# A two-part transformer kernel: scaled activations split straight from x, and SBUF tiles placed at chosen distances modulo 512 bytes

## The chip, the cores and the metric

One core of one Trainium2 chip. The metric is the device time of one execution in microseconds, median of three runs. Everything is computed on one NeuronCore; weights, 353 MB of them with the other inputs, are streamed from HBM once.

## The reference

Two blocks in sequence on x of 256 positions by 1024 features in fp32, each block with two layers. Cut to what matters here:

```
# first block, per layer
x = x + 0.5 * swiglu(rmsnorm(x, ffn1_norm), w_up, w_down)
x = x + mixer(rmsnorm(x, mix_norm), ...)      # attention, conv module, gates, w_out
x = x + 0.5 * swiglu(rmsnorm(x, ffn2_norm), w_up, w_down)
x = rmsnorm(x, final_norm)
# second block, per layer
p = rmsnorm(x, norm1) @ w_in                  # K, Q, V and the Fourier part
x = x + concat(rmsnorm(fourier), rmsnorm(attention)) @ w_o
x = x + (silu(gate) * val) @ w_down           # of conv3(rmsnorm(x, norm2) @ w_up)
```

## The kernel before

**Precision by parts.** Each product of activations and weights is made of three matmuls in fp32r. A number is split into a high part (rounded to fp32r) and a low part (the rest). `mm3` (lines 443 to 445) multiplies w_hi by a_hi, w_hi by a_lo and w_lo by a_hi, in this order, into one PSUM bank. Each matmul loads its own weights first (128 by 128) and moves 256 columns of activations. While a matmul moves its columns, the weights of the next are loaded.

**The weight stream.** SyncE loads chunks of 2048 fp32 per partition (half of that for some) into `raw`, with three slots. ScalarE copies a chunk into `hi` (line 1066), VectorE writes `lo` = `raw` - `hi` (line 1618), and TensorE works through it: 48 matmuls on a full chunk, 24 on a half one. A slot of `hi` and `lo` is free when TensorE is done with it, a slot of `raw` when VectorE has written `lo`.

**The stages.** In each of the six feed-forward blocks (FFN) TensorE takes 33 chunks: the moving tiles are `n_hi` and `n_lo` for the way up, `hid_hi` and `hid_lo` for the way down, and `last_*` and `end_*` for the last chunks down. A layer of the first block then has value chunks (moving 512 columns of weights), eight GLU chunks, twelve of queries and keys, two of values, eight of gates (moving tiles `h_hi`, `h_lo`), the projections (`yt_*`, `s_*`) and w_out (`h_*` again). The second block's projection w_o also moves `h_*`. While the queries, keys and gates are computed, VectorE makes the depthwise convolution of 31 taps on 8 tiles: `conv_taps` is a generator of single taps, and the constants `TAPS_GLU`, `TAPS_QK`, `TAPS_V` and `TAPS_HEAD` say how many are made in each step. `TAPS_HEAD[t]` belongs to step t of the gate stage, in which one pair of heads is also attended to.

**The seams.** Where a matmul chain ends in x, `add_to_x` (line 1719) adds two PSUM halves to a pair p of x's eight tiles. The next norm's gain is applied to x, and the result is split: VectorE writes x times gain into a wide tile (`scale_x`, line 1677; `fused_scale`, line 1662, with two gains where the final norm lies between), ScalarE copies it to `n_hi` (`scaled_high`, line 1111), VectorE subtracts (`scaled_low`, line 1622). The division by the root mean square comes later, out of the PSUM bank, so TensorE can start on a pair of `n_hi` and `n_lo` as soon as it is there. ScalarE also squares x for the statistic (`squares`, line 1115), and at the two fused seams, behind the first block's layers, makes a second set of squares (`psq`, line 1098). There are 40 such pairs; the 8 ahead of the mixer keep the wide tile, since it is used again.

**The layout.** `sb` (in `build`) hands out SBUF addresses one behind the other, in multiples of 64 bytes. All tiles that matter here have rows of a multiple of 512 bytes, so each has one distance modulo 512 from the base of `hi`: before, `raw`, `lo`, `x`, `h_hi`, `h_lo` and `sq` are at 0, `last_*` and `end_*` at 128, `n_*`, `hid_*`, `s_*` and `yt_*` at 192.

Of the kernel before, what the change touches and what calls it, by code (L numbers as in the profile page):

```python
# [20 lines left out]
F32 = mybir.dt.float32  # L21
# [9 lines left out]
L = 2  # L31
# [13 lines left out]
TAPS_HEAD = (14, 12, 16, 20, 20, 8 * 31, 0, 0)  # L45
# [155 lines left out]
def _stream(chunks):  # L201
    return dict(hi=chunks, lo=chunks, pe=chunks, slot=chunks, load0=16 * chunks // 3,
                load1=16 * chunks // 3, load2=16 * chunks // 3)


def _ffns(n):
    return dict(half=n * (PAIRS - 1), up=n * JT, silu=n * JT, prod=n * JT, hidhi=n * JT, hid=n * JT,
                dpair=3 * n)
# [4 lines left out]
    added2=16 * ADDED_IN[2], x=12, sq=12, stat=3, std=3, h32=16, hhi=16, h=16, prm=1,  # L213
# [5 lines left out]
    _stream(CHUNKS2), **_ffns(1), x=8, sq=8, ssum=2, stat=2, std=2, h32=8, hhi=8, h=8, prm=1,  # L219
# [5 lines left out]
class Semaphores:  # L225
# [6 lines left out]
             "yf", "fsum", "fstat", "fstd", "mf", "wo", "fgain", "psq", "plink", "psum", "pstat", "pstd", "minus", "added0", "added1", "added2")  # L232


def build(nc, d):
# [61 lines left out]
    spread = sb("spread", [P, 2 * ROWS * HD], F32, at_u + (KT * UPW + KT * S) * 4 + 10240)  # L297
    at_t = state["at"]
# [44 lines left out]
    nmx, den, rden, fgain, nsink = (small[:, 16 * i:16 * i + 16] for i in range(5))  # L343

# [707 lines left out]
    def act_program(act):  # L1052
# [33 lines left out]
        def fused_input(p, l):  # L1086

            scaled_high(p)
            take("x")
            if l == 0 and p == 0:  # L1090
                act.wait_ge(sem["fgain"], L + 1)
            for t in (2 * p, 2 * p + 1):
                out, src = xsq[:, t, :], x[:, t, :]
                if l == L - 1:
                    out, src = natural(out), evens_first(src)
                last = fn(out, src, ACT.Square, scale=fgain[:, l * KT + t:l * KT + t + 1])
            last.then_inc(sem["sq"], 1)
            fn(psq[:, 2 * p:2 * p + 2, :], x[:, 2 * p:2 * p + 2, :], ACT.Square).then_inc(sem["psq"], 1)
# [13 lines left out]

        def squares(p):
            take("x")
            fn(xsq[:, 2 * p:2 * p + 2, :], now["x"][:, 2 * p:2 * p + 2, :], ACT.Square).then_inc(sem["sq"], 1)

        def projection(c0, half):

            for m in range(KT):
                split(c0 + m + 2, half(c0 + m + 2))  # L1120
                take("pe")
                if m % 2 == 0 and m:
                    scaled_input(m // 2 - 1)
            scaled_input(3)
# [118 lines left out]
        def first_inputs():  # L1243

            scaled_high(0)
            first_high(0)
            scaled_high(1)
            first_high(1)
            scaled_high(2)
            scaled_high(3)  # L1250
            act.wait_ge(load[1], 16)
            fn(hi[:, 1, :], raw[:, 1, :], ACT.Copy).then_inc(sem["hi"], 1)
            for p in range(4):
                squares(p)
            take("prm")

        def layer1(l):
            if l == 0:
                first_inputs()
            else:  # L1260
                for p in range(4):
                    fused_input(p, l - 1)
                take("prm")
# [215 lines left out]

        def layer2(l):  # L1480
            for p in range(4):
                if l == 0:
                    fused_input(p, L - 1)
                else:
                    scaled_input(p)
# [77 lines left out]
            scaled_input(0)  # L1563
            take("pe")
            split(B_FFN0)
            scaled_input(1)
            take("pe")
            split(B_FFN0 + 1)
            scaled_input(2)
            take("pe")  # L1570
            scaled_input(3)
# [23 lines left out]
    def dve_program(v):  # L1595
# [57 lines left out]
        def fused_scale(p, l):  # L1653

            take("x")
            at = l * NP1 + P1["final"]
            next_at = (l + 1) * NP1 + P1["ffn1"] if l < L - 1 else L * NP1 + P2["norm1"]
            for t in (2 * p, 2 * p + 1):
                out, part = sq[:, t, :], x[:, t, :]
                if l == L - 1:  # L1660
                    out, part = natural(out), evens_first(part)
                last = v.tensor_scalar(out, part, prm_all[:, at + t:at + t + 1], prm_all[:, next_at + t:next_at + t + 1],
                                       ALU.mult, ALU.mult)
            last.then_inc(sem["h32"], 1)

        def gain_of(table, gain, t):
            if table is P2 and gain == "norm1":
                at = L * NP1 + now["layer"] * NP2 + P2["norm1"] + t
                return prm_all[:, at:at + 1]
            return col(table, gain, t)  # L1670

        def scale_x(p, table, gain):

            take("x")
            for j in range(2):
                t = 2 * p + j
                last = v.tensor_scalar(now["wide"][:, t, :], now["x"][:, t, :], gain_of(table, gain, t), None, ALU.mult)  # L1677
            last.then_inc(sem["h32"], 1)

        def scaled_low(p):  # L1680
            take("hhi")
            low_part(n_lo[:, 2 * p:2 * p + 2, :], now["wide"][:, 2 * p:2 * p + 2, :], n_hi[:, 2 * p:2 * p + 2, :], "h")

# [72 lines left out]
        def projection(c0, half, factor, table, gain):  # L1756

            for m in range(KT - 1):
                split(c0 + m + 2, half(c0 + m + 2))
                if m % 2:  # L1760
                    v.wait_ge(sem["pe"], pe_after(c0 + m))
                    add_to_x(OUT_BANKS[m // 2], m // 2, factor)
                    scale_x(m // 2, table, gain)
                elif m:
                    scaled_low(m // 2 - 1)
            v.wait_ge(sem["pe"], pe_after(c0 + KT - 1))
            add_to_x(OUT_BANKS[3], 3, factor)
            scale_x(3, table, gain)
            split(c0 + KT + 1, half(c0 + KT + 1))
            scaled_low(3)  # L1770
# [121 lines left out]
        def first_inputs():  # L1892

            def arrived(p):
                v.wait_ge(sem[f"xld{p}"], 16)
                v.sem_inc(sem["x"], 1)
                scale_x(p, P1, "ffn1")

            v.wait_ge(sem["gains"], 16)
            arrived(0)  # L1900
            scaled_low(0)
            arrived(1)
            first_low(0)
            scaled_low(1)
            arrived(2)
            first_low(1)
            scaled_low(2)
            arrived(3)
            scaled_low(3)
            v.wait_ge(sem["hi"], 2)  # L1910
            v.tensor_tensor(lo[:, 1, :], raw[:, 1, :], hi[:, 1, :].bitcast(F32), ALU.subtract).then_inc(sem["lo"], 1)
            v.wait_ge(sem["prmld"], 16)
            v.tensor_copy(prm[:, 0:NP1], prm_all[:, 0:NP1]).then_inc(sem["prm"], 1)
            v.wait_ge(sem["prm"], 1)

        def layer1(l):
            start["pe"] = cnt.at("pe")

            if l:
                v.tensor_copy(prm[:, 0:NP1], prm_all[:, l * NP1:(l + 1) * NP1]).then_inc(sem["prm"], 1)  # L1920
                take("prm")
            else:
                cnt.up("prm")
            roped["rope"] = cnt.at("rope")
# [144 lines left out]
            projection(WOUT0, half_chunk_1, 0.5, P1, "ffn2")  # L2069
# [14 lines left out]
        def ffn2(cb):  # L2084
# [57 lines left out]
            if now["layer"] < L:  # L2142
                scaled_residual(c + 6, 1.0, P2, "norm1")
            else:
                residual(c + 6, 1.0)
                cnt.up("x", 4)
                cnt.up("hhi", 4)
# [74 lines left out]

        def pair_done(p):
            add_to_x(OUT_BANKS2[p], p, 1.0)
            scale_x(p, P2, "norm2")

        def layer2(l):
# [91 lines left out]
            scaled_low(0)  # L2319
# [3 lines left out]
            scaled_low(1)  # L2323
# [4 lines left out]
            scaled_low(2)  # L2328
            scaled_low(3)
# [222 lines left out]
```

## Time and profile before

| | us |
|---|---|
| median of three runs | 1968.24 |
| the three runs | 1968.24, 1966.21, 1976.1 |
| the profiled execution, its own time | 1977.89 |
| its span, first to last instruction | 1976.1 |
| TensorE busy in the span | 1928.1 |
| VectorE busy | 1498.7 |
| ScalarE busy | 1082.2 |

The profile is of one execution, which took 1977.89 us, 9.65 us more than the median of the runs. TensorE's busy time holds overlaps: a matmul's record lasts about 0.28 us although the next starts some 0.12 us after it, so the pace of matmuls is read from their starts, or from their number in a stretch.

### The profile page before, as it was taken

What the parts mean: (1) busy time and instruction counts of PE and PEld (TensorE: products, weight loads), DVE (VectorE), ACT (ScalarE), POOL (GpSimd) and SP (SyncE); (2) the same over time, 40 slices, a digit from 0 to 9 for tenths busy, and PEclk for the clock granted to TensorE, in tenths of its full rate; (3) what the DMA queues carried; (4) which work ended last, traced back from release to release, by engine and by line L of the source; (5) the groups of instructions that cost most, each with busy time, mean ns of one, the idle gap of its engine ahead of it and who ended that gap; (6) DMA issues with size and microseconds to landing.
All of it is one profiled execution on the core that took longest, in us unless ns stands there. A gap on an engine that the chain in (4) does not pass through costs nothing.

```text
span 1976.1 us, 38819 instructions
## 1 busy us (share of the span) xinstructions
PE 1928.1 (98%) x15828; PEld 1857.7 (94%) x15828; DVE 1498.7 (76%) x2189; ACT 1082.2 (55%) x1370; POOL 31.4 (2%) x40
## 2 busy tenths in 40 slices
PE   6999999999999999999999999999999999999998
PEld 6999899889999999998988899999889999889998
DVE  6555889987765586668898877555888778879777
ACT  4444556666544464445666665444665555566554
POOL 0000001000000000000110000000000000000000
PEclk9999999999999999999999999999999999999999
DMA  6556579634655545555896246555335554435554
GB/s 240 204 183 227 184 236 275 173 89 140 212 194 189 191 162 200 191 209 187 256 257 171 84 149 227 198 179 188 110 126 192 191 191 171 138 130 175 187 187 143
DMA packets 61003, 362.28 MB, mean 183 GB/s; under 512 B 7904, under 2 KB 8160, under 8 KB 24160
## 3 DMA queue, kind: packets, MB, share of 16 engines
q1 hardware_dynamic: 54704, 339.37, 49.5%
q0 software_dynamic: 5184, 18.88, 5.5%
q10 hardware_dynamic: 1008, 2.51, 0.3%
q8 instruction: 79, 1.29, 0.3%
q14 instruction: 28, 0.23, 0.0%
HBM read 353.39 MB, written 1.05 MB: 179 GB/s over the span
## 4 chain that ended last, share of the span: by engine, by line
PE 76%; DVE 15%; ACT 5%; DMA 2%; issue 1%; DVEq 0%; ACTq 0%; SPq 0%
PE bank L443 24%; PE bank L444 23%; PE bank L445 23%; DVE lo L1618 5%; DVE cv L1862 3%; ACT hi L1066 2%; DMA raw<-in_w 1%; DVE n_lo L1622 1%; PE bank L585 1%; DMA x<-in_x 1%; DMA lo<-in_w 1%; DVE p_sb L1841 1%; PE bank L607 0%; DVE up_t L1698 0%; DVE sq L1677 0%
## 5 line engine op out<-in xcount | busy, mean ns | idle before, releaser
L1618 DVE TENSOR_TENSOR lo<-raw,hi 128x2048 fp32r<-128x2048 f32 (+1 forms) x336 | 676.6, 2015 | 203.0 <-ACT hi L1066 202.5
L443 PE MATMUL bank<-n_hi,hi 128*128 128x256 f32 x2256 | 638.2, 283 | 24.7 <-DVE lo L1889 12.7
L1066 ACT ACTIVATE hi<-raw 128x2048 fp32r<-128x2048 f32 (+1 forms) x336 | 598.3, 1783 | 110.5 <-PE bank L445 92.2
L444 PE MATMUL bank<-n_lo,hi 128*128 128x256 f32 x2256 | 631.3, 280 | 0.0
L445 PE MATMUL bank<-n_hi,lo 128*128 128x256 f32 x2256 | 631.1, 280 | 0.0
L443 PEld LDWEIGHTS bank<-n_hi,hi 128*128 128x128 f32 x2256 | 427.9, 190 | 31.5 <-DVE lo L1889 12.7
L444 PEld LDWEIGHTS bank<-n_lo,hi 128*128 128x128 f32 x2256 | 426.6, 189 | 1.3 <-issue 1.0
L445 PEld LDWEIGHTS bank<-n_hi,lo 128*128 128x128 f32 x2256 | 426.5, 189 | 0.0
L443 PE MATMUL bank<-h_hi,hi 128*128 128x256 f32 x1152 | 335.9, 292 | 5.0 <-DVE h_lo L1622 4.3
L444 PE MATMUL bank<-h_lo,hi 128*128 128x256 f32 x1152 | 327.1, 284 | 0.0
L445 PE MATMUL bank<-h_hi,lo 128*128 128x256 f32 x1152 | 326.9, 284 | 0.0
L443 PE MATMUL bank<-hid_hi,hi 128*128 128x256 f32 x928 | 259.5, 280 | 0.5 <-DVE lo L1618 0.5
L445 PE MATMUL bank<-hid_hi,lo 128*128 128x256 f32 x928 | 259.2, 279 | 0.0
L444 PE MATMUL bank<-hid_lo,hi 128*128 128x256 f32 x928 | 259.2, 279 | 0.0
L443 PEld LDWEIGHTS bank<-h_hi,hi 128*128 128x128 f32 x1152 | 221.7, 192 | 17.9 <-issue 12.6
L444 PEld LDWEIGHTS bank<-h_lo,hi 128*128 128x128 f32 x1152 | 222.2, 193 | 0.5
L445 PEld LDWEIGHTS bank<-h_hi,lo 128*128 128x128 f32 x1152 | 222.0, 193 | 0.0
L1132 ACT ACTIVATE silu_t<-up_t 128x256 f32<-128x256 f32 x88 | 36.8, 418 | 298.3 <-DVE up_t L1698 298.3
L1862 DVE SCALAR_TENSOR_TENSOR cv<-upad,prm,cv 128x256 f32<-128x256 f32 x480 | 195.4, 478 | 0.0
L443 PEld LDWEIGHTS bank<-hid_hi,hi 128*128 128x128 f32 x928 | 175.5, 189 | 0.9 <-DVE lo L1618 0.9
L444 PEld LDWEIGHTS bank<-hid_lo,hi 128*128 128x128 f32 x928 | 174.9, 189 | 0.0
L445 PEld LDWEIGHTS bank<-hid_hi,lo 128*128 128x128 f32 x928 | 174.8, 188 | 0.0
(257 smaller groups left out, 2302.4 us busy)
## 6 DMA issues: line engine op xcount, KB each, us to landing
raw<-in_w SPq DMA_DIRECT2D x286, 1024.0 KB, 4.8
raw<-in_w SPq DMA_DIRECT2D x53, 512.0 KB, 4.0
lo<-in_w POOLq DMA_DIRECT2D x36, 512.0 KB, 9.0
zt<-zt SPq DMA_DIRECT2D x96, 64.0 KB, 5.8
bv<-in_bv SPq DMA_DIRECT2D x2, 768.0 KB, 6.1
spread<-in_spread SPq DMA_DIRECT2D x2, 768.0 KB, 8.0
x<-in_x ACTq DMA_DIRECT2D x4, 256.0 KB, 10.4
out_x<-sq SPq DMA_DIRECT2D x1, 1024.0 KB, 3.9
```

Of the source, the lines that this page charges most:

```text
L443: mm(out, w_hi, a_hi, start=start, stop=False, skip_group_check=True)
L444: mm(out, w_hi, a_lo, start=False, stop=False, skip_group_check=True)
L445: return mm(out, w_lo, a_hi, start=False, stop=True, skip_group_check=True)
L585: last = mm(bank[7][j * HD:(j + 1) * HD, 0:S], const[:, w:w + HD], zgsq[:, j, :], start=(m == 0), stop=(m == QK_CHUNKS - 1), skip_group_ch ...
L1066: fn(hi[:, s, 0:w], raw[:, s, 0:w], ACT.Copy).then_inc(sem["hi"], 1)
L1132: fn(silu_t[:, u, :], gate_of[:, u, 0, :], ACT.Silu).then_inc(sem["silu"], 1)
L1618: v.tensor_tensor(lo[:, s, 0:w], raw[:, s, 0:w], hi[:, s, 0:w].bitcast(F32), ALU.subtract)\
L1622: return v.tensor_tensor(out, full, high.bitcast(F32), ALU.subtract).then_inc(sem[name], 1)
L1841: v.tensor_tensor_reduce(p_sb[:, e, :], bank[3 + e][:, :], mask_f[:, u % 2, :], -(HD ** -0.5), 3e38, ALU.add, ALU.min, nmx[:, i:i + 1]).th ...
L1862: ins = v.scalar_tensor_tensor(cv[:, t, :], src, w, cv[:, t, :], ALU.mult, ALU.add)
```

## The change

It has four parts.

1. **Layout.** `lo` moves to 256 modulo 512 from `hi`; `x`, `h_hi`, `h_lo` and `sq` move to 192; `z`, `zt`, `p_sb`, `last_*`, `end_*` and what shares their place move from 128 to 192. `raw`, `hi`, `n_*`, `hid_*`, `s_*`, `yt_*`, and the constants stay where they were modulo 512.
2. **Parts straight from x.** For 32 of the 40 pairs the wide tile is gone: `direct_high` makes `n_hi` as x times gain on ScalarE, in two instructions of one tile each, and `direct_low` makes `n_lo` as (x times gain) minus `n_hi` on VectorE, again in two. The product of the two gains of a fused seam, `seam_gain`, is computed once at the start, by two small instructions on VectorE.
3. **Order on ScalarE at the fused seams.** The squares of pair p come behind the high part of pair p+1, and the second squares (`psq`) behind all of them.
4. **Taps.** `TAPS_HEAD` goes from (14, 12, 16, 20, 20, rest) to (14, 12, 16, 18, 18, 18, rest).

The programs of TensorE, SyncE and GpSimd are the same instructions in the same order.

```diff
-TAPS_HEAD = (14, 12, 16, 20, 20, 8 * 31, 0, 0)
+TAPS_HEAD = (14, 12, 16, 18, 18, 18, 8 * 31, 0)
...
     raw = sb("raw", [P, SLOTS, CW], F32)
     hi = sb("hi", [P, SLOTS, CW], F32R)
+    state["at"] += 256
     lo = sb("lo", [P, SLOTS, CW], F32R)
+    state["at"] += 256
+    state["at"] += 192
     x = sb("x", [P, KT, S], F32)
     h_hi = sb("h_hi", [P, KT, S], F32R)
     h_lo = sb("h_lo", [P, KT, S], F32R)
     sq = sb("sq", [P, KT, S], F32)
+    state["at"] += 320
     const = sb("const", [P, C["mask1"]], F32)
...
     spread = sb("spread", [P, 2 * ROWS * HD], F32, at_u + (KT * UPW + KT * S) * 4 + 10240)
+    state["at"] += 64
     at_t = state["at"]
...
+        def fused_inputs(l):
...
+            for p in range(4):
+                direct_high(p, x, lambda t: seam_gain[:, l * KT + t:l * KT + t + 1], l == L - 1)
+                if p:
+                    final_squares(p - 1)
+            final_squares(3)
+            for p in range(4):
+                fn(psq[:, 2 * p:2 * p + 2, :], x[:, 2 * p:2 * p + 2, :], ACT.Square).then_inc(sem["psq"], 1)
...
+        def direct_high(p, src, gain, in_order=False):
+
+            take("x")
+            for t in (2 * p, 2 * p + 1):
+                out, part = n_hi[:, t, :], src[:, t, :]
...
+                last = fn(out, part, ACT.Copy, scale=gain(t))
+            last.then_inc(sem["hhi"], 1)
...
+        def direct_low(p, src, gain, in_order=False):
+
+            take("x")
+            take("hhi")
+            for t in (2 * p, 2 * p + 1):
+                out, part, high = n_lo[:, t, :], src[:, t, :], n_hi[:, t, :].bitcast(F32)
...
+                last = v.scalar_tensor_tensor(out, part, gain(t), high, ALU.mult, ALU.subtract)
+            last.then_inc(sem["h"], 1)
...
         def fused_residual(c, factor, l):
+
+            def low(p):
+                direct_low(p, x, lambda t: seam_gain[:, l * KT + t:l * KT + t + 1], l == L - 1)
...
                 add_to_x(2 + p, p, factor)
-                fused_scale(p, l)
                 if p:
-                    scaled_low(p - 1)
-            scaled_low(3)
+                    low(p - 1)
+            low(3)
```

The other places (`projection`, `direct_residual`, the second block's four pairs ahead of its FFN, and the first inputs) are changed in the same way.

On VectorE, at the seam behind the first layer, the rows before, from the first `add_to_x` to the first low part (the last three rows stand twice more, and then one more low part):

```order
L1719 SCALAR_TENSOR_TENSOR x<-bank,x 128x512
L1662 TENSOR_SCALAR sq<-x,prm_all 128x256 x2
L1719 SCALAR_TENSOR_TENSOR x<-bank,x 128x512
L1662 TENSOR_SCALAR sq<-x,prm_all 128x256 x2
L1622 TENSOR_TENSOR n_lo<-sq,n_hi 128x512
```

and in the changed kernel:

```order
L1746 SCALAR_TENSOR_TENSOR x<-bank,x 128x512 x2
L1708 SCALAR_TENSOR_TENSOR n_lo<-x,small,n_hi 128x256 x2
L1746 SCALAR_TENSOR_TENSOR x<-bank,x 128x512
L1708 SCALAR_TENSOR_TENSOR n_lo<-x,small,n_hi 128x256 x2
L1746 SCALAR_TENSOR_TENSOR x<-bank,x 128x512
L1708 SCALAR_TENSOR_TENSOR n_lo<-x,small,n_hi 128x256 x4
```

The four scalings are gone, and each low part is two instructions of one tile that read x, the gain (in `small`) and `n_hi`; the second `add_to_x` follows the first at once.

On ScalarE at the same seam, the last two chunks of the FFN and the first pair before (the other three pairs are alike):

```order
L1066 ACTIVATE hi<-raw 128x2048 x2
L1111 ACTIVATE n_hi<-sq 128x512
L1096 ACTIVATE xsq<-x,small 128x256 x2
L1098 ACTIVATE psq<-x 128x512
L1111 ACTIVATE n_hi<-sq 128x512
```

and all of it in the changed kernel, with the chunk that follows:

```order
L1134 ACTIVATE n_hi<-x,small 128x256 x4
L1103 ACTIVATE xsq<-x,small 128x256 x2
L1134 ACTIVATE n_hi<-x,small 128x256 x2
L1103 ACTIVATE xsq<-x,small 128x256 x2
L1134 ACTIVATE n_hi<-x,small 128x256 x2
L1103 ACTIVATE xsq<-x,small 128x256 x4
L1112 ACTIVATE psq<-x 128x512 x4
L1072 ACTIVATE hi<-raw 128x2048
```

The high parts of the first two pairs now come ahead of any squares, and `psq` moved from between the pairs to their end, ahead of the copy of the next chunk.

On VectorE in the first layer's gate stage, the head of step 6 before (steps 3 to 5 end in runs of 20, 20 and 18 taps, `SCALAR_TENSOR_TENSOR cv<-upad,prm,cv`; the ISA rows are the minima over scores and their read-out):

```order
L1618 TENSOR_TENSOR lo<-raw,hi 128x2048
L1846 RECIPROCAL small<-small 128x2
L1841 ISA p_sb,small<-bank,mask_f 128x512
L1841 ISA small 128x1
L1841 ISA p_sb,small<-bank,mask_f 128x512
```

and in the changed kernel (where steps 3 to 5 have 18, 18 and 18):

```order
L1653 TENSOR_TENSOR lo<-raw,hi 128x2048
L1885 RECIPROCAL small<-small 128x2
L1901 SCALAR_TENSOR_TENSOR cv<-upad,prm,cv 128x256 x4
L1880 ISA p_sb,small<-bank,mask_f 128x512
L1880 ISA small 128x1
```

Four taps moved behind the reciprocal of step 6.

## Rows read from the trace of the kernel before

**Rows 1.** Page: engines, granted clock in 40 slices, chain's shares

```profile
PE 1928.1 (98%) x15828; PEld 1857.7 (94%) x15828; DVE 1498.7 (76%) x2189; ACT 1082.2 (55%) x1370; POOL 31.4 (2%) x40
...
PEclk9999999999999999999999999999999999999999
...
PE 76%; DVE 15%; ACT 5%; DMA 2%; issue 1%; DVEq 0%; ACTq 0%; SPq 0%
```

**Rows 2.** Windows, TensorE: stretch, us, busy us (instructions), clock, DMA share, GB/s

```profile
40.00:190.00 150.00, 150.00 (x1274) 1.00 0.58 204
540.00:690.00 150.00, 150.00 (x1276) 1.00 0.55 191
735.00:870.00 135.00, 135.00 (x1193) 1.00 0.58 207
1220.00:1370.00 150.00, 150.00 (x1276) 1.00 0.55 194
1525.00:1655.00 130.00, 130.00 (x1150) 1.00 0.56 198
1815.00:1955.00 140.00, 140.00 (x1191) 1.00 0.54 185
230.00:270.00 40.00, 40.00 (x334) 1.00 0.56 188
1158.00:1170.00 12.00, 12.00 (x108) 1.00 0.66 206
1960.00:1970.00 10.00, 10.00 (x86) 1.00 0.07 29
```

**Rows 3.** Timeline at 750 us: start us, us, engine, line, operation

```profile
749.91 0.19 PEld L444 LDWEIGHTS bank<-n_lo,hi 128*128 128x128 f32 x1
750.02 0.28 PE L444 MATMUL bank<-n_lo,hi 128*128 128x256 f32 x1
750.03 0.19 PEld L445 LDWEIGHTS bank<-n_hi,lo 128*128 128x128 f32 x1
```

**Rows 4.** Windows, all engines: PE, PEld, DVE, ACT, POOL, then as above

```profile
272.00:345.00 73.00, 73.00 (x586) 67.63 (x586) 67.94 (x128) 50.30 (x65) 9.50 (x11) 1.00 1.02 283
382.00:428.00 46.00, 44.76 (x391) 41.49 (x390) 43.22 (x104) 31.50 (x55) 2.59 (x3) 1.00 0.49 123
490.00:514.00 24.00, 23.56 (x196) 23.36 (x196) 16.77 (x25) 11.64 (x14) 0.00 (x0) 1.00 0.72 230
```

**Rows 5.** Timeline of VectorE at the second seam

```profile
1390.46 0.68 DVE L1719 SCALAR_TENSOR_TENSOR x<-bank,x 128x512 f32<-128x512 f32 x1
1391.17 0.74 DVE L1662 TENSOR_SCALAR sq<-x,prm_all 128x256 f32<-128x256 f32 x2
1391.83 0.68 DVE L1622 TENSOR_TENSOR n_lo<-sq,n_hi 128x512 fp32r<-128x512 f32 x1
1392.82 0.69 DVE L1622 TENSOR_TENSOR n_lo<-sq,n_hi 128x512 fp32r<-128x512 f32 x1 [0.31 <-ACT n_hi L1111]
1393.43 2.28 DVE L1618 TENSOR_TENSOR lo<-raw,hi 128x2048 fp32r<-128x2048 f32 x1
```

**Rows 6.** Timeline of ScalarE there

```profile
1392.17 0.61 ACT L1111 ACTIVATE n_hi<-sq 128x512 fp32r<-128x512 f32 x1
1392.69 0.92 ACT L1096 ACTIVATE xsq<-x,small 128x256 f32<-128x256 f32 x2
1393.51 0.61 ACT L1098 ACTIVATE psq<-x 128x512 f32<-128x512 f32 x1
```

**Rows 7.** Waits of TensorE on `n_lo`: us, times, longest

```profile
PE bank L443 <- DVE n_lo L1622: 5.5, 8, 1.7
```

**Rows 8.** Chain of waits in a gate stage: start us, us, what

```profile
415.78 7.91 DVE cv L1862 x20
...
427.19 7.12 DVE cv L1862 x18
...
438.61 1.27 PE bank L635 x8
```

More of the change, by code:

```diff
@@ L1084, in final_gains, with final_squares @@
             fn(fgain, fgain, ACT.Sqrt, bias=eps).then_inc(sem["fgain"], 1)
[L1086 to L1090, printed above, removed]
+        def fused_inputs(l):
+            if l == 0:
                 act.wait_ge(sem["fgain"], L + 1)
[L1092 to L1098, printed above, removed]
+                act.wait_ge(sem["seam"], L)
+            def final_squares(p):
+                for t in (2 * p, 2 * p + 1):
+                    out, src = xsq[:, t, :], x[:, t, :]
+                    if l == L - 1:
+                        out, src = natural(out), evens_first(src)
+                    last = fn(out, src, ACT.Square, scale=fgain[:, l * KT + t:l * KT + t + 1])
+                last.then_inc(sem["sq"], 1)
+            for p in range(4):
[5 more added lines that the diff above has]
+                fn(psq[:, 2 * p:2 * p + 2, :], x[:, 2 * p:2 * p + 2, :], ACT.Square).then_inc(sem["psq"], 1)
         def final_std(out, src, seam):
@@ L1111, in scaled_high, with direct_input @@
             fn(n_hi[:, 2 * p:2 * p + 2, :], now["wide"][:, 2 * p:2 * p + 2, :], ACT.Copy).then_inc(sem["hhi"], 1)
+        def direct_high(p, src, gain, in_order=False):
+            take("x")
+            for t in (2 * p, 2 * p + 1):
+                out, part = n_hi[:, t, :], src[:, t, :]
+                if in_order:
+                    out, part = natural(out), evens_first(part)
+                last = fn(out, part, ACT.Copy, scale=gain(t))
+            last.then_inc(sem["hhi"], 1)
+        def direct_input(p, gain):
+            direct_high(p, now["x"], gain)
+            fn(xsq[:, 2 * p:2 * p + 2, :], now["x"][:, 2 * p:2 * p + 2, :], ACT.Square).then_inc(sem["sq"], 1)
         def squares(p):
@@ L1260, in layer1 @@
             else:
-                for p in range(4):
-                    fused_input(p, l - 1)
+                fused_inputs(l - 1)
                 take("prm")
@@ L1651, in final_scale @@
                 last.then_inc(sem["plink"], 1)
[L1653 to L1670, printed above, removed]
         def scale_x(p, table, gain):
@@ L1676, in scale_x @@
                 t = 2 * p + j
-                last = v.tensor_scalar(now["wide"][:, t, :], now["x"][:, t, :], gain_of(table, gain, t), None, ALU.mult)
+                last = v.tensor_scalar(now["wide"][:, t, :], now["x"][:, t, :], col(table, gain, t), None, ALU.mult)
             last.then_inc(sem["h32"], 1)
@@ L1682, in scaled_low @@
             low_part(n_lo[:, 2 * p:2 * p + 2, :], now["wide"][:, 2 * p:2 * p + 2, :], n_hi[:, 2 * p:2 * p + 2, :], "h")
+        def direct_low(p, src, gain, in_order=False):
+            take("x")
+            take("hhi")
+            for t in (2 * p, 2 * p + 1):
+                out, part, high = n_lo[:, t, :], src[:, t, :], n_hi[:, t, :].bitcast(F32)
+                if in_order:
+                    out, part, high = natural(out), evens_first(part), natural(high)
+                last = v.scalar_tensor_tensor(out, part, gain(t), high, ALU.mult, ALU.subtract)
+            last.then_inc(sem["h"], 1)
         def summed_squares():
@@ L1754, in scaled_residual, with direct_residual, projection @@
             scaled_low(3)
-        def projection(c0, half, factor, table, gain):
+        def direct_residual(c, factor, gain):
+            for p in range(4):
+                if p < 3:
+                    take("dpair")
+                else:
+                    v.wait_ge(sem["pe"], pe_after(c))
+                add_to_x(2 + p, p, factor)
+                if p:
+                    direct_low(p - 1, now["x"], gain)
+            direct_low(3, now["x"], gain)
+        def projection(c0, half, factor, gain):
             for m in range(KT - 1):
@@ L1923, in layer1 @@
                 cnt.up("prm")
+                for m in range(L):
+                    at = m * NP1 + P1["final"]
+                    next_at = (m + 1) * NP1 + P1["ffn1"] if m < L - 1 else L * NP1 + P2["norm1"]
+                    v.tensor_tensor(seam_gain[:, m * KT:(m + 1) * KT], prm_all[:, at:at + KT],
+                                    prm_all[:, next_at:next_at + KT], ALU.mult).then_inc(sem["seam"], 1)
+                v.wait_ge(sem["seam"], L)
             roped["rope"] = cnt.at("rope")
@@ L2142, in ffn2 @@
             if now["layer"] < L:
-                scaled_residual(c + 6, 1.0, P2, "norm1")
+                at = L * NP1 + now["layer"] * NP2 + P2["norm1"]
+                direct_residual(c + 6, 1.0, lambda t: prm_all[:, at + t:at + t + 1])
             else:
@@ L2327, in layer2 @@
             pair_done(3)
-            scaled_low(2)
-            scaled_low(3)
+            direct_low(2, now["x"], norm2)
+            direct_low(3, now["x"], norm2)
             split(B_FFN0 + 1)
```

71 lines of the change are left out of this document (37 added, 34 removed).

## The prediction

> **What bounds the kernel now.** I read the page first, then TensorE's pace in windows, then the timeline for one pair of matmuls, and last the waits and the chain around the places that the change edits.
>
> TensorE is busy 98% of the span, has the full clock in every slice, and holds 76% of the chain that ended last [rows 1]. Waiting is a small part of the time, so the question is how fast TensorE goes while it does not wait. The windows of rows 2 answer that. A window also counts about two matmuls that started before it (a record is 0.28 us long), so I divide by the count less two. Every matmul in these windows moves 256 columns and loads 128 by 128 weights, yet there are three paces:
>
> - 117.8 ns in four of the six FFNs (windows at 40, 540, 1220 and 1815 us: 150 us / 1272 and alike), 113.3 ns in the other two (735 and 1525) and in the stage of `s_*` (1158): all of them move tiles at distance 192 from the base of `hi`;
> - 120.5 ns in the GLU stage (230), which moves `h_*` at distance 0;
> - 119 ns at the end (1960), where `last_*` and `end_*` lie at distance 128 [rows 2].
>
> The pace of an FFN holds through the whole block, whichever slot of weights is in use. Within a pace, the next weights start loading 10 ns after a matmul's start, and the matmul after starts when they are in [rows 3]: the two streams of reads run side by side all the time, and their relative place sets how much they cost each other. That is my reading. The trace shows no address, only that equal work has three paces and that the tile's distance goes with them. At 192 there are two paces, and which one holds looks like a matter of how the two streams fell in step after the last wait.
>
> **The layout, h and last tiles.** Moving `h_*` to 192 gives 120.5 - 113.3 = 7.2 ns per matmul if it takes the fast pace, 2.7 ns if the slow one, nothing if distance is not the cause.
> - GLU: 2 layers x 8 chunks x 48 = 768 matmuls, fast: 5.5 us.
> - Queries and keys: 2 x 12 x 48 = 1152, fast 8.3 us. VectorE is busy 67.94 of 73 us there and the DMA engines all of the time [rows 4]. Taking 4.1 us out of 73 would bring VectorE to 98.6%, so I count half: 4.2 us.
> - Gates: VectorE is busy 43.22 of 46 us [rows 4] and its taps are on the chain [rows 8]. Nothing from the pace.
> - w_out: the DMA share is 0.72 with half chunks [rows 4], and its chunks come late. I count nothing there, and half of 384 x 7.2 for w_o: 1.5 us.
> - `last_*` and `end_*`: 384 matmuls x (119 - 113.3) = 2.2 us.
>
> **The layout, low weights.** `lo` goes to 256. Then the matmuls that load high weights keep distance 192, and those that load low weights, one in three, get 192 - 256, which is 448 modulo 512. No row shows 448. The bounds come from rows 2: at best all three go at 113.3, at worst that one goes at 120.5 and takes the others to 117.8, or 118.7 on average. The jump of 256 comes twice in every three loads, so two streams that fell in step badly are put out of step again each time, while the fast pace costs the two streams nothing that a jump could take away. I take the fast pace, with doubt. Some 6,000 matmuls of the four slow FFNs are past their first, waiting chunks: 6,000 x (117.8 - 113.3) = 27.0 us. This is the largest term and the least certain one.
>
> The Trainium skill speaks against all of this: in "SBUF — State Buffer", section "Who interferes with whom", it gives TensorE two independent read ports and says that TensorE never waits on anyone. By that rule both layout terms are zero and the sum is 6.7 us. Rows 2 do not fit it: same work, same clock, 113.3 to 120.5 ns.
>
> **The seams.** A pair cost VectorE 0.68 + 0.74 + 0.68 us before, with starts 1.98 us apart per pair [rows 5]. It will cost the 0.68 us of `add_to_x` and two fused operations of one tile. Twenty taps of that kind and size take 7.91 us [rows 8], 0.40 each, so 0.8 us for two. That is 1.5 us per pair: about 0.5 less, 16 us of VectorE in all 32 pairs, nearly all beside TensorE's work. ScalarE pays: a copy of 0.61 us becomes two scaled ones, and the nearest row has two scaled squares at 0.92 [rows 6], so 0.3 more per pair, 10 us in all, under 55% load [rows 1]. At the fused seams `psq` now lies ahead of the next chunk's copy, but the pairs are earlier by more than it costs.
> What of this is on the path: TensorE waits for `n_lo` 8 times, 5.5 us in total [rows 7], and VectorE goes on serially to the next chunk's low part [rows 5] and the sum of squares. Following the new order through the second seam, the last low part ends 1.4 us earlier (four pairs at 0.5 less, less 0.6 since TensorE's own pairs now set the start), the first fused seam 1.3, the second block's inner seam 0.8, the two projections 0.2 each and the two w_o seams 0.3 each. Sum 4.5 us. The first inputs have the longer high part and the two small products in a serial chain: +0.4. Net 4.1 us. Ends: 0 (another wait takes its place) and the 5.5 of rows 7 plus the same again.
>
> **The taps.** In the gate stage the chain goes from 20 taps to 18 to a wait of TensorE [rows 8]. Four taps leave steps 3 and 4 (2 each), none is added to step 5, which had 18 of the rest anyway, and four come in step 6, after the last wait. That is 4 x 0.40 = 1.6 us per layer. They end near the sum over the tiles that needs them, so I count 1.3: 2.6 us.
>
> **The sum.** 27.0 + 5.5 + 4.2 + 1.5 + 2.2 + 4.1 + 2.6 = 47.1 us. Against the profiled execution's own time: 1977.9 - 47.1 = 1930.8, say **1931 us**. That execution is 9.7 us above the median of 1968.2. If its four slow FFNs are more than other runs have, my term is smaller against the median but ends at the same place, since all blocks are then fast. So 1931 stands for the median too.
>
> **The rivals.**
> - *The low part's shift does nothing* (0.30): if the streams meet again every 256 bytes or less, 448 is the same as 192. For it: the tiles at 0 and at 128 have nearly one pace [rows 2], which looks like a short period. Then FFNs fall to either pace as before, `h_*` and the last tiles too. The h terms shrink to about 4 of 7.2 ns: 3.1 + 2.3 + 0.8 + 1.2, with seams and taps 14.1 us: 1963.8 against the profiled execution, 1954.1 against the median. Named time: 1959.
> - *Slower: the low weights' matmuls go badly* (0.15): 448 is 64 from 0, and the pace at 0 is the worst one known [rows 2]. Today's mean over the 13,700 matmuls concerned is 117.3 ns (6336 at 117.8, 3456 at 120.5, 384 at 119, the rest 113.3). It decides above 117.8 ns, where it eats the 6.7 us of seams and taps. At 118.7 it costs 1.4 x 13,700 = 19 us less 6.7: 1990 against the profiled execution; half of that gives 1984, and 1974 against the median.
> - *Distance is not the cause* (0.10): the stage of `h_*` is slow for another reason, say its other traffic. Against it is rows 2, where `s_*`, at another distance in the same layer, goes at 113.3. Only the 6.7 us of seams and taps stay: 1971 against the profiled execution, 1962 against the median. The rule of the Trainium skill quoted above comes out here.
>
> **How the numbers follow.** My forecast has 0.45, with its own range 1921 (queries and keys gain in full, seams at their upper end) to 1943 (a fifth of the FFN term and half of the others missing). About 0.5%, or 10 us, is what a measurement can tell from no change: faster is under 1958.4, slower over 1978.1. Faster: 0.45, half of 0.30, and 0.03 of the rest: 0.63. Slower: 0.12 of the second rival. Same: 0.25. The range reaches from 1921 through the first and the last rival to 1970, leaving out mostly the second.
>
> **What would show it.** Right: every long FFN window at 113 ns, GLU there too, `n_lo` waits below 3 us, the last low part of the second seam 1.4 us closer to its first `add_to_x`, VectorE's busy time down by some 16 us and ScalarE's up by 10. Wrong: FFN windows still split between 113 and 118 (first rival), any steady pace above 118 (second), GLU still at 120.5 (third).

## The result and the profile after

| | before | after |
|---|---|---|
| median, us | 1971.08 (11 runs, 1966.21 to 1977.08) | 1960.52 (11 runs, 1952.08 to 1968.35) |
| profiled execution, its own time, us | 1977.89 | 1954.6 |
| its span, us | 1976.1 | 1952.8 |

The ratio of after to before is 0.9936, 95% interval 0.9918 to 0.9955: faster by 0.64%, or 10.6 us between the medians and 23.3 us between the profiled executions. The forecast was 47.1 us and 1931 us; the first rival (the shift of the low weights does nothing) had named 1959.

The page's lines for engines, clock and chain [rows 1]:

```profile
PE 1903.9 (97%) x15828; PEld 1833.5 (94%) x15828; DVE 1484.9 (76%) x2159; ACT 1091.1 (56%) x1402; POOL 31.4 (2%) x40
...
PEclk9999999999999999999999999999999999999999
...
PE 72%; DVE 19%; ACT 4%; DMA 3%; issue 2%; SPq 0%; DVEq 0%; ACTq 0%
```

VectorE's busy time fell by 13.8 us and ScalarE's rose by 8.9, about as forecast (16 and 10), and the clock is as before. TensorE's busy time fell by 24.2 us.

The windows of TensorE's pace answer to [rows 2] (stretch, us, busy us with the number of matmuls, clock, DMA share, GB/s): the six FFNs in order, then GLU, `s_*`, and the end tiles.

```profile
40.00:190.00 150.00, 150.00 (x1276) 1.00 0.58 205
530.00:680.00 150.00, 150.00 (x1275) 1.00 0.54 189
720.00:860.00 140.00, 139.59 (x1231) 1.00 0.58 203
1210.00:1360.00 150.00, 150.00 (x1276) 1.00 0.55 191
1510.00:1640.00 130.00, 130.00 (x1150) 1.00 0.56 199
1795.00:1930.00 135.00, 135.00 (x1193) 1.00 0.57 196
230.00:268.00 38.00, 37.82 (x333) 1.00 0.60 200
1145.00:1157.00 12.00, 12.00 (x108) 1.00 0.69 207
1937.00:1946.00 9.00, 8.65 (x75) 1.00 0.12 52
```

The FFNs still have the two paces, 117.8 ns (150 us / 1274) and 113.3 to 113.9. Three are slow instead of four. GLU went from 120.5 to 114.8 ns by the window (38 us / 331, small waits included), and the last tiles from 119 to 118.5 or less (8.65 us / 73). The mean distance of starts inside blocks, with waits left out, says it sharper. Outside the gates, where attention comes in between, `h_*` had 119.8 to 119.9 ns before in all six stretches, and has 113.3 to 117.8 after: the two stretches of w_o, in the second block, took the slow pace. `last_*` and `end_*` of the last FFN together had 119.9 before and have 115.5 after.

The second seam on VectorE [rows 5], its first row before:

```profile
1385.13 0.68 DVE L1719 SCALAR_TENSOR_TENSOR x<-bank,x 128x512 f32<-128x512 f32 x1
```

and after:

```profile
1370.94 0.68 DVE L1746 SCALAR_TENSOR_TENSOR x<-bank,x 128x512 f32<-128x512 f32 x1
1372.05 0.69 DVE L1746 SCALAR_TENSOR_TENSOR x<-bank,x 128x512 f32<-128x512 f32 x1 [0.42 <-PE bank L451]
1372.70 0.88 DVE L1708 SCALAR_TENSOR_TENSOR n_lo<-x,small,n_hi 128x256 fp32r<-128x256 f32 x2
...
1377.05 0.88 DVE L1708 SCALAR_TENSOR_TENSOR n_lo<-x,small,n_hi 128x256 fp32r<-128x256 f32 x2 [0.68 <-ACT n_hi L1134]
```

and on ScalarE [rows 6]:

```profile
1375.23 0.92 ACT L1103 ACTIVATE xsq<-x,small 128x256 f32<-128x256 f32 x2
1376.03 0.91 ACT L1134 ACTIVATE n_hi<-x,small 128x256 fp32r<-128x256 f32 x2
```

From the start of the first `add_to_x` to the end of the last low part it took 8.38 us before (1385.13 to 1393.51) and takes 6.99 (1370.94 to 1377.93): 1.39 us less, where 1.4 was forecast. The last low part now waits for ScalarE, which spends 0.92 + 0.91 us per pair; a pair's low part is 0.88 us on VectorE, not 0.8. TensorE's waits on low parts of `n` [rows 7] went from 8 times, 5.5 us, to:

```profile
PE bank L449 <- DVE n_lo L1657: 2.0, 1, 2.0
...
PE bank L449 <- DVE n_lo L1708: 1.2, 4, 0.6
```

That is 3.2 us in all, where the forecast's sign was below 3. Other waits grew: on `lo` from 6.7 us to

```profile
PE bank L449 <- DVE lo L1653: 8.2, 10, 1.4
```

The chain in the first gate stage [rows 8]:

```profile
412.17 7.12 DVE cv L1901 x18
...
422.79 7.12 DVE cv L1901 x18
...
434.21 1.27 PE bank L641 x8
```

The long runs of taps are 7.12 us each, so the one of 7.91 is shorter by 0.79. What TensorE's faster pace did in the stage of queries and keys is seen in the windows of all engines (columns as in [rows 4]):

```profile
272.00:343.00 71.00, 68.79 (x571) 62.70 (x569) 65.78 (x124) 50.06 (x64) 8.64 (x10) 1.00 1.01 276
```

TensorE was busy in all of its window before, and now stands still for 2.2 of 71 us; VectorE is at 93% and the DMA engines still at all of the time. The chain changed hands. Its shares there, before (272 to 345 us):

```profile
by line: PE bank L443 32.1%; PE bank L444 29.6%; PE bank L445 29.5%; PE bank L585 7.2%; PE bank L596 1.7%
```

After, the transfers of `zt` hold 29.6% of the chain in 272 to 345 us, where they had no share before. Three of its pieces (start us, us, what):

```profile
279.96 10.36 DMA zt<-zt
290.34 1.24 DVE zt L1864
...
312.27 11.27 DMA zt<-zt
```

**Where the time went.** Stage lengths from the starts of records, the two layers of the first block (GLU from its first matmul to its last sigmoid, queries and keys to the last copy of `zt`, gates from there to the last `yt_hi`):

| stage, us | before | after | layout alone | parts and taps alone |
|---|---|---|---|---|
| GLU | 46.4, 46.3 | 44.2, 43.8 | 44.2, 43.8 | 46.4, 46.3 |
| queries, keys | 79.2, 80.0 | 78.8, 77.9 | 76.8, 76.3 | 79.1, 79.1 |
| gates | 101.7, 101.7 | 100.7, 101.8 | 101.8, 101.7 | 100.1, 100.1 |
| w_out, to the next FFN's first matmul | 25.6, 24.0 | 23.3, 23.3 | 24.9, 24.0 | 23.5, 24.1 |

The difference of the two spans is 23.3 us. GLU gave 4.7, queries and keys 2.5, gates 0.9, w_out 3.0, the stretches behind the two fused seams (their start to the next `h` matmul) 1.4 and 1.5, the second block's inner seam 0.8, w_o 1.2, the start with the first FFN 0.8, in sum 16.8. The last FFN gave 5.5 (176.8 to 171.3, up to its `last_*` tiles), and this need not be the change's: e8 below shows the same step in the kernel before. The last 1.0 us is spread over the rest.

### The profile page after: what moved, and what is told of

It is laid out like the page before. It is cut to its first block, busy times and chain, and to the rows that moved or that the text cites. A ratio compares the mean times of both kernels' runs of the same rounds, so it can differ in the third digit from the quotient of the medians.

```text
span 1952.8 us, 38855 instructions
## 1 busy us (share of the span) xinstructions
PE 1903.9 (97%) x15828; PEld 1833.5 (94%) x15828; DVE 1484.9 (76%) x2159; ACT 1091.1 (56%) x1402; POOL 31.4 (2%) x40
## 4 chain that ended last, share of the span: by engine, by line
PE 72%; DVE 19%; ACT 4%; DMA 3%; issue 2%; SPq 0%; DVEq 0%; ACTq 0%
PE bank L449 23%; PE bank L450 22%; PE bank L451 22%; DVE lo L1653 6%; DVE cv L1901 5%; DMA zt<-zt 2%; ACT hi L1072 1%; DVE zt L1864 1%; ACT n_hi L1134 1%; DMA raw<-in_w 1%; DVE qk L1874 1%; DVE p_sb L1880 1%; PE bank L613 0%; DVE c L2122 0%; DVE c L2118 0%
## 5 line engine op out<-in xcount | busy, mean ns | idle before, releaser
L449 PE MATMUL bank<-h_hi,hi 128*128 128x256 f32 x1152 | 330.1, 287 | 7.3 <-DVE h_lo L1657 3.9
L451 PE MATMUL bank<-h_hi,lo 128*128 128x256 f32 x1152 | 321.1, 279 | 0.0
L450 PE MATMUL bank<-h_lo,hi 128*128 128x256 f32 x1152 | 321.1, 279 | 0.0
L450 PEld LDWEIGHTS bank<-h_lo,hi 128*128 128x128 f32 x1152 | 217.9, 189 | 0.5
```

The costliest lines, as they stand in the source:

```text
L449: mm(out, w_hi, a_hi, start=start, stop=False, skip_group_check=True)
L450: mm(out, w_hi, a_lo, start=False, stop=False, skip_group_check=True)
L451: return mm(out, w_lo, a_hi, start=False, stop=True, skip_group_check=True)
```

## The experiments

All numbers "per block" are mean distances of the starts of neighbouring matmuls of 256 columns, waits left out, from the trace of the profiled execution; those of `h_*` leave out the gates. e4 to e11 and e13 to e15 are single executions, on several chips, so their paces say more than their times: single executions of the kernel before beside e5 to e11 took 1970.84 and 1980.69 us.

**e1: layout alone.** The kernel before with the four shifts of the change.

```diff
# before.py
+    state["at"] += 256      # ahead of lo
+    state["at"] += 448      # ahead of x
+    state["at"] += 320      # ahead of const
+    state["at"] += 64       # ahead of z
```

> The kernel before with the layout part of the change alone (lo at 256, h, x, sq and the last tiles at 192). Theory 1, distance sets the pace and the low part's shift does nothing: GLU windows at 113.3 or 117.8 ns instead of 120.5, FFN blocks still at either 113.3 or 117.8, time 5 to 9 us below the kernel before. Rival, the tiles' distance is not the cause and all of the change's gain is its shorter seams and taps: GLU still at 120.5 and no difference in time.

1962.54 us, ratio 0.9929 (0.9903 to 0.9954). FFNs: 117.7, 117.6, 113.8, 117.7, 117.6, 113.8 ns; `h_*` 113.3 to 114.2 in five stretches and 117.8 in one. So the move of the `h` tiles works, and four FFNs are slow again.

**e2: parts and taps alone.** The changed kernel with the old layout.

```diff
# after.py
-    state["at"] += 256
...
-    state["at"] += 256
-    state["at"] += 192
...
-    state["at"] += 320
...
-    state["at"] += 64
```

> The changed kernel with the old layout: the parts straight from x, the order on ScalarE and the taps alone. Theory 1: GLU at 120.5 ns again, the two fused seams as short as in the changed kernel, time 4 to 8 us below the kernel before. Rival, the gain is the layout's alone: no difference to the kernel before.

1966.57 us, ratio 0.9945 (0.9918 to 0.9972). `h_*` is at 119.8 to 119.9 ns everywhere, where e1 has the fast pace in them: together they end the rival that distance is not the cause. Four of the six FFNs are slow here too (117.6 to 117.7 ns). The gates give 1.6 us per layer (table above), which is the taps' 4 x 0.40; parts and taps were not run apart.

**e3: no shift of the low weights.** The changed kernel with `lo` at 0; all else stays at its place.

```diff
-    state["at"] += 256
     lo = sb("lo", [P, SLOTS, CW], F32R)
-    state["at"] += 256
     state["at"] += 192
```

> The changed kernel with lo at 0 instead of 256 modulo 512, all else as in it. Theory 1, the shift does nothing: the same two paces, the same time as the changed kernel within 4 us. Rival, the shift helps some blocks into the fast pace: more blocks at 117.8 and a time 5 us or more above the changed kernel; or it hurts: a time below it.

1955.27 us, ratio 0.9902 (0.9881 to 0.9923), no worse than with the shift. The FFNs: 113.4, 117.8, 117.8, 117.6, 113.5, 113.6 ns. Three are slow, as in the changed kernel, and the two profiled executions took 1955.24 and 1954.6 us. The shift by 256 bought nothing. The medians are 5.3 us apart, more than the 4 us expected; whether the shift even costs something is open. The first, second and third FFN:

```profile
40.00:190.00 150.00, 150.00 (x1326) 1.00 0.59 211
530.00:680.00 150.00, 150.00 (x1276) 1.00 0.55 190
720.00:860.00 140.00, 140.00 (x1191) 1.00 0.57 199
```

**e4 to e7: the distance by itself.** All moving tiles at one distance D, `lo` at 0, with 256, 64, 448, 128 for D.

```diff
     hi = sb("hi", [P, SLOTS, CW], F32R)
-    state["at"] += 256
     lo = sb("lo", [P, SLOTS, CW], F32R)
-    state["at"] += 256
-    state["at"] += 192
+    state["at"] += D
```

The pad of 320 ahead of `const` stays as it is, and carries `n_*`, `hid_*` and all later moving tiles from 192 to D as well. The constants and other tiles shift with them.

> The changed kernel with lo at 0 and every moving tile at distance 256 from hi (one look, for the pace). If the two streams of reads meet again every 256 bytes or less, 256 is the same as 0: all blocks at 120.5 ns, time near 2000 us. If they meet every 512 bytes, 256 is the farthest from 0: a pace of its own, at 113.3 or below, time under 1950 us.

> All moving tiles at 64 modulo 512 from hi, lo at 0, parts and taps as changed. Theory A (the streams meet again every 256 bytes, and the distance from a meeting decides): 64 has the same distance as 192 on the other side; paces of 113.3 and 117.8 ns per block again, about 1955 to 1962 us. Theory B (the sign counts, moving tile ahead of the weights by 64 is worse or better): one single pace, between 110 and 120 ns, in every block: at 113.3 everywhere 1925 to 1935 us, at 119 to 120 about 1995 us.

> All moving tiles at 448 modulo 512 from hi, lo at 0. Theory A (period 256): the same as 192, so FFN blocks and h blocks at 113.3 or 117.8 ns and 1952 to 1965 us. Theory B (period 512): another pace than at 192, at worst 120 ns and 2000 us. This is the distance that the low weights' matmuls have in the change.

> All moving tiles at 128 modulo 512 from hi, lo at 0. Theory A (period 256, 128 is furthest from a meeting): like last_* and end_* of the kernel before, 118.7 to 119.9 ns everywhere, about 1990 us. Theory B (the distance from a meeting alone decides, the further the faster): below 117 ns everywhere, under 1950 us.

| D | time, us | paces per block, ns |
|---|---|---|
| 256 | 2000.0 | 120.0 in every FFN, 119.8 to 120.0 in `h_*` |
| 64 | 1969.4 | 117.8 in five FFNs, 113.7 in one; `s_*` 117.8 and 113.3 |
| 448 | 1963.0 | 117.6, 117.6, 117.6, 117.7, 113.5, 113.8 |
| 128 | 1988.3 | 118.7 in five FFNs, 120.0 in one |

The windows of D = 256 at 40 and 535 us, 150 us / 1250 = 120.0 ns:

```profile
40.00:190.00 150.00, 150.00 (x1252) 1.00 0.57 203
535.00:685.00 150.00, 150.00 (x1252) 1.00 0.54 187
```

and of D = 128, the first FFN and the fifth (150 us / 1264 = 118.7 ns; 130 us / 1084 = 119.9):

```profile
40.00:190.00 150.00, 150.00 (x1266) 1.00 0.57 204
...
1515.00:1645.00 130.00, 130.00 (x1086) 1.00 0.53 183
```

256 acts as 0 (119.8 to 120.5 ns), 448 as 192. So the pace repeats after 256 bytes. 64 and 192 share the two paces 113.3 and 117.8; 0 and 128 never have the fast one. That makes the change's `lo` at 256 a null step: 448 is 192.

**e8: the kernel before, once more.**

> The kernel before, once more, for its paces. Theory A (which of the two paces a block takes is settled anew in each execution): four slow and two fast FFNs need not come again, another set of blocks is fast, and the time moves by 3 to 7 us for each block (1584 matmuls x 4.5 ns = 7.1 us at most). Theory B (the program fixes it): the same blocks, 117.4, 117.7, 113.7, 117.7, 113.5, 117.3 ns.

1970.75 us. Five FFNs took the same paces as in the first profile, the sixth took 113.5 ns instead of 117.3:

```profile
1220.00:1370.00 150.00, 150.00 (x1276) 1.00 0.56 193
1525.00:1655.00 130.00, 130.00 (x1150) 1.00 0.56 198
1810.00:1945.00 135.00, 135.00 (x1193) 1.00 0.56 195
```

The span is 7.1 us shorter, 5.7 of it in this block (171.1 us instead of 176.8). So a block's pace is partly settled anew in each execution, and the forecast counted from a profiled execution that may have had one slow FFN more than the next.

The starts of single matmuls say when the pace is settled. In the eight profiled executions whose FFNs show both paces (before, e8, after, e1, e2, e3, e5, e6), a block changes between 113.3 and 117.8 ns only straight behind a wait. With the pace read over 12 starts and a wait taken as a distance of starts above 135 ns, there are 78 changes in 48 blocks, each within four matmuls of a wait. The last wait comes behind matmul 193 of 1536 or 1488 at the latest, and the pace it leaves holds to the end of the block. In the second and fourth FFN that last wait is 305 ns from start to start, and all 16 of these blocks went on slowly; in the other four FFNs both outcomes occur. The third FFN of the kernel before shows one such change, in 8 us on either side of a wait on `lo` (8 us / 68 = 117.6 ns, then 8 us / 71 = 112.7):

```profile
721.30:729.30 8.00, 8.00 (x70) 1.00 0.34 131
730.40:738.40 8.00, 8.00 (x73) 1.00 0.66 213
...
730.10 0.36 PE L443 MATMUL bank<-n_hi,hi 128*128 128x256 f32 x1 [0.33 <-DVE lo L1618]
```

The work of the other engines does not matter: in the kernel before, the first FFN has 117.7 to 117.9 ns and the third 113.3, whether VectorE, ScalarE, both or neither is at work at the moment.

**e9: the low weights at 128.** The changed kernel with a jump of half of 256 in place of the whole.

```diff
-    state["at"] += 256
+    state["at"] += 128
     lo = sb("lo", [P, SLOTS, CW], F32R)
-    state["at"] += 256
-    state["at"] += 192
+    state["at"] += 64
```

> The low weights at 128 instead of 256, moving tiles at 192, parts and taps as changed: one matmul in three now has distance 64 instead of 192, a jump of half of the 256 bytes after which the streams meet again. Theory A (my prediction's mechanism, with the right size of jump: a real jump puts the streams out of a bad step): every FFN near 113.3 ns, 1930 to 1938 us. Theory B (the state outlives the jump, since 64 has the same two paces): blocks at 113.3 and 117.8 ns, 1952 to 1970 us. Theory C (each jump costs): a steady pace above 117.8 ns, over 1970 us.

1935.87 us, beside 1980.69 of the kernel before on the same chip. The six FFNs in windows:

```profile
40.00:190.00 150.00, 150.00 (x1326) 1.00 0.59 212
524.00:674.00 150.00, 150.00 (x1325) 1.00 0.56 196
706.00:844.00 138.00, 137.23 (x1211) 1.00 0.55 194
1196.00:1346.00 150.00, 150.00 (x1325) 1.00 0.56 197
1492.00:1622.00 130.00, 130.00 (x1150) 1.00 0.57 199
1777.00:1912.00 135.00, 135.00 (x1193) 1.00 0.56 196
```

All six FFNs have the fast pace, 113.3 ns (150 us / 1324), 113.5 in the one with a wait in its window; `h_*` 113.3 to 113.9. Theory A's outcome came: the forecast's step gives what it promised, with another number of bytes. Whether the jump puts the streams out of a slow step, or the two distances 192 and 64 together have no slow pace to fall into, the trace cannot tell.

**e10, e11: between the steps of 64.** All moving tiles at 160 and at 224, the edit as in e4.

> All moving tiles at 160 modulo 512 from hi, lo at 0: between 128 (118.7 and 120.0 ns) and 192 (113.3 and 117.8 ns). Theory A (a smooth dependence on the distance): a pace between, 115 to 119 ns in every block, 1955 to 1985 us. Theory B (only whole steps of 64 count): the paces of 128 or of 192, unchanged.

> All moving tiles at 224 modulo 512 from hi, lo at 0: between 192 (113.3 and 117.8 ns) and 256 (120.0 ns). Theory A (a smooth dependence): between 115 and 120 ns in every block. Theory B (only whole steps of 64 count): the paces of 192 or of 256, unchanged. If 113.3 ns holds in every block, about 1930 us, this is the distance to use.

1987.09 and 1981.78 us. 160 has 118.6 or 119.9 ns in five FFNs and 117.5 in the last, 224 has 118.3 in every block. Neither has the fast pace, so 192 is not one point on a slope towards something better. Between the two, 224 lies between its neighbours 192 and 256; 160 lies near 128.

**e12: the low weights at 128, timed.** The edit of e9 again.

> The kernel of the look at lo = 128 again, timed. Theory A (the jump of half a period drives every block out of the slow pace in every execution): all FFNs at 113.3 to 113.5 ns again, median 1930 to 1938 us, spread of the runs below 8 us, ratio to before 0.978 to 0.984. Theory B (the look was luck, the pace of each block is still open): blocks at 117.8 ns come back, median 1945 to 1958 us with a spread of 10 us or more.

1940.78 us (six runs, 1935.97 to 1943.64), ratio 0.9831 (0.9789 to 0.9874), where before spread from 1959.94 to 1987.5 in eleven. All six FFNs were at 113.4 ns again. The median is 3 us above the expected band, and the spread just inside 8 us.

**e13: the jump alone.** The kernel before with `lo` at 128 and nothing else.

```diff
# before.py
+    state["at"] += 128
     lo = sb("lo", [P, SLOTS, CW], F32R)
+    state["at"] += 384
```

> The kernel before with the low weights at 128 and nothing else changed. Theory A (the jump alone makes the fast pace): all six FFNs at 113.4 ns, the h blocks at 119 to 120 as before (distances 0 and 128, neither with the fast pace), and 1978 - 27 = 1951 us against the profiled execution of before, or 1971 - 21 = 1950 us against one with only three slow FFNs. Theory B (the parts straight from x or the h tiles have a share in it): FFNs at 117.7 ns remain and 1960 to 1978 us.

1951.98 us. The six FFNs in windows, then GLU with `h_*` still at 0:

```profile
40.00:190.00 150.00, 150.00 (x1324) 1.00 0.60 211
530.00:680.00 150.00, 150.00 (x1326) 1.00 0.57 196
710.00:850.00 140.00, 139.22 (x1229) 1.00 0.55 195
1205.00:1355.00 150.00, 150.00 (x1326) 1.00 0.58 198
1505.00:1635.00 130.00, 130.00 (x1149) 1.00 0.56 199
1790.00:1925.00 135.00, 135.00 (x1193) 1.00 0.57 196
230.00:268.00 38.00, 38.00 (x321) 1.00 0.62 212
```

Against the profile of before the four slow FFNs went from 186.0, 181.8, 181.9 and 176.8 us to 180.0, 175.3, 175.3 and 171.1: 24.8 us, by two lines of padding. GLU stays slow, at 119.1 ns (38 us / 319).

**e14: the low weights at 384.** As e9 with 384 in place of 128 (and 320 ahead of `x`).

> The changed kernel with the low weights at 384. Theory A (period of 256): 384 is 128, all blocks at 113.4 ns, 1932 to 1940 us. Theory B (period of 512 or none): 113.3 and 117.8 ns mixed, 1950 to 1965 us.

1938.9 us, all six FFNs 113.4 ns. 384 acts as 128.

**e15: the low weights at 64.** As e9 with 64 (and 128 ahead of `x`): two matmuls in three at distance 192, one at 128.

> The changed kernel with the low weights at 64: two matmuls in three at distance 192 and one at 128, where all matmuls together take 118.7 or 120.0 ns. Theory A (any real jump throws the streams out of the slow step and the fast one costs nothing): 113.4 ns, 1932 to 1940 us. Theory B (each matmul pays by its own distance): (2 x 113.4 + 118.7) / 3 = 115.2 ns in every block, 1955 to 1965 us. Theory C (the bad distance pulls the others along): 117.8 ns or more, over 1975 us.

1981.07 us and 118.2 ns in every block:

```profile
40.00:190.00 150.00, 150.00 (x1271) 1.00 0.58 205
535.00:685.00 150.00, 150.00 (x1272) 1.00 0.54 190
```

No state is left to chance here, but the pace is the wrong one: a third of the matmuls at a distance without a fast pace goes with 118.2 ns for all, where theory C had expected 117.8 or more. Of the pairs of distances tried, the jump helped where both have the fast pace by themselves (192 and 64), and not where one has not (192 and 128 here, 0 and 128 in e13's `h_*`).

## Why the forecast was wrong

**The low weights' shift, 27.0 us: failed.** This is the step "The jump of 256 comes twice in every three loads, so two streams that fell in step badly are put out of step again each time". 256 bytes are no jump. With `lo` at 0 (e3) the blocks have the same two paces as with `lo` at 256, and tiles at 256 and 448 behave as tiles at 0 and 192 (e4, e6). The first rival had this and its argument: the tiles at 0 and at 128 have nearly one pace, "which looks like a short period". That clue was in [rows 2] and I put it second. The part of the step that says "which one holds looks like a matter of how the two streams fell in step after the last wait" stands: all 78 changes of pace come behind a wait (e8). The size of the term was right too: the same step with 128 bytes gave 24.8 us in the FFNs (e13, one execution), and the whole kernel with it stands at 1940.8 us in the median (e12), 1935.9 in e9, where 1931 was forecast.

**The profiled execution as the base: weak.** One of its four slow FFNs was fast in the next profile of the same program (e8). The text said that the forecast did not hang on this, since all blocks would be fast; once they were not, it did.

**A reading of [rows 3]: wrong.** The prediction says that the next matmul starts when its weights are in. Its load is recorded from 750.03 to 750.22 us, and the matmul starts before that:

```profile
750.14 0.28 PE L445 MATMUL bank<-n_hi,lo 128*128 128x256 f32 x1
```

No term hung on it.

**GLU, 5.5 us: right,** 4.7 measured. The starts put the old pace at 119.8 to 120.0 ns rather than 120.5, which leaves 5.0 us of the term. The stage took a little above the fast pace, 114.2 and 114.6 ns over all of `h_*` before the projections.

**Queries and keys, 4.2 us: right in kind.** Layout alone gives 6.1 us over both layers, the whole change 2.5. Taking a part off for VectorE and the transfers was needed, since TensorE now waits there for `zt` and `qk`. How much of a gain survives differs from one execution to the next (79.7 and 79.1 us in e12, 77.8 and 77.3 in e9; the kernel before has 79.2 and 80.0, in e8 79.7 and 79.2); why, I did not separate.

**Taps, 2.6 us: about right alone, given back in the whole.** Parts and taps give 3.2 us in the gates (e2), but the whole change 0.9, on its two layers 1.0 and -0.1. In this stage VectorE's taps are the chain, so time that the earlier stages saved is waited for here. That reading fits the rows; it was not tested by itself.

**w_out, nothing: too low,** 3.0 measured against one profile, 2.8 against the mean of two (24.7 us per layer in e8). The layout alone leaves the stage at 24.9 and 24.0, so nothing from the pace was right; parts and taps bring it to 23.5 and 24.1, and only both to 23.3 twice. **w_o, 1.5: about right by luck,** 1.2 measured. Half of 384 x 7.2 ns is 1.4 us, and the half was meant for late chunks at the fast pace. Both stretches took the slow pace (117.8 and 117.7 ns), which is worth 0.8 us; what gave the rest was not read apart. **The end tiles, 2.2: two thirds came.** In the last two FFNs they went from 118.7 and 119.9 ns to 113.5 and 115.5, which over 96 matmuls each is 0.9 us. In the other four they followed their block's pace, 117.8 ns in three and 113.3 in one, which is 0.5 us more.

**Seams, 4.1 us: right where they can be read apart.** 1.39 us at the second one (1.4 forecast), 1.4 at the first (1.3), 0.8 at the inner one (0.8). The 1.0 us of the projections and w_o is inside those stages. The start did not cost its 0.4: the first FFN began no later.

Outside the low weights' term 20.1 us were forecast, and 16.8 came in the stages listed above.

The Trainium skill ("SBUF — State Buffer", section "Who interferes with whom") gives TensorE two independent read ports, one for the moving tile and one for the weights, and says that TensorE never waits on anyone. For other engines the trace agrees: the pace is the same with and without VectorE and ScalarE at work (e8). That the reads of the two ports cost each other nothing does not fit these matmuls, though the trace does not show the reads themselves: e13 moves one tile of weights and nothing else modulo 512, and all FFNs take the fast pace. e4 and e9, the same program but for padding, took 2000.0 and 1935.9 us, one execution each, with the clock at 1.00 in every window shown.

The two halves of the change do not add up in the medians, each compared with the kernel before of its own session: 0.71% for the layout, 0.55% for parts and taps, 0.64% together. The gates give back a part. The rest may be the throw of the FFNs' paces, some 6 us each, which stays in a median of few runs; that was not settled.

## What to carry to other kernels

When equal matmuls show more than one pace in one trace at a full clock, treat the place of the moving tile against the weights' tile as a parameter to vary, and find the period first, by one kernel with everything moved by a suspected period: had e4 stood ahead of the design, `lo` would not have been put at 256. Where a pace has two states, a layout can be chosen that leaves no choice: here moving tiles at 192 from the high weights and the low weights 128 further, with a ratio of 0.9831 to the kernel before against the 0.9936 of the change as made, the two intervals apart. Look at the starts of single matmuls behind the waits, where the pace is settled. And do not read one profiled execution as the program: profile it twice before a term is counted in blocks.

## What the runs showed of the hardware

- A matmul of 256 columns in fp32r with its own load of 128 by 128 weights goes on at 113.3 to 120.0 ns, at a granted clock of 1.00, by the distance of its moving tile from the weights' tile modulo 256 bytes (from the code; the trace shows no address) and, at some distances, by how it came out of the last wait. At 0: 120.0. At 64 and 192: 113.3 or 117.8. At 128: 118.7 or 120.0. At 160: 118.6 or 119.9, in one FFN 117.5. At 224: 118.3.
- At 64 and 192 the pace changes only straight behind a wait (78 changes of 78, in eight executions) and otherwise holds, here for some 1,300 matmuls or more (150 us). It can differ between two executions of one program (e8), and does not depend on whether VectorE or ScalarE is at work.
- An alternation of distances 192 and 64, with one matmul in three at the second, was fast in all 24 FFNs of the four profiles that have it (e9, e12, e13, e14). 192 with 128 was at 118.2 ns in all six of e15.
- Why the distance matters, no run here shows.
